# Attention heads on TensorE: mask as contraction rows, output product from high and low halves

## The reference

```python
mask = cid[None, :ke] <= cid[s0:e0, None]           # cid: 0 for meta tokens, then 1 per 64 tokens
sc = jnp.einsum('bqhcd,bkhcd->bhcqk', q[:, s0:e0], k[:, :ke])     # c = 0, 1; d = 64
p = jax.nn.softmax(jnp.where(mask, sc, -jnp.inf), axis=-1)
attn = p[:, :, 0] - lam * p[:, :, 1]
outs.append(jnp.einsum('bhqk,bkhe->bqhe', attn, v[:, :ke]))        # e = 128
```

## Time and profile before

| | us |
|---|---|
| median of 3 runs | 1306.67 (1305.73 to 1308.74) |
| profiled execution, first to last instruction | 1303.2 |
| PE busy | 1278.0 (98%) |
| PE weight loads busy | 1153.7 (89%) |
| DVE busy | 682.4 (52%) |
| ACT busy | 544.9 (42%) |
| POOL busy | 65.8 (5%) |
| attention, from the first scores to the last output product | 674.2 to 900.0 |

### The profile page before, as it was taken

One profiled execution on the slowest core, in us unless ns is written; L12 is line 12 of the kernel. 1 busy time (PEld: TensorE's weight loads), 2 busy tenths in 40 slices (PEclk: granted clock), 3 DMA queues, 4 the chain that ended last, 5 costly groups with the idle time before them and its releaser, 6 DMA issues.

```text
span 1303.2 us, 20870 instructions
## 1 busy us (share of the span) xinstructions
PE 1278.0 (98%) x8381; PEld 1153.7 (89%) x8381; DVE 682.4 (52%) x992; ACT 544.9 (42%) x895; POOL 65.8 (5%) x90
## 2 busy tenths in 40 slices
PE   7999999999999999999999999998999999999997
PEld 6899999999999999999988888876888888888886
DVE  5877777654334334234556677663643343443443
ACT  4656655543214123123445566664532241231332
POOL 3321221000000000000000000000000000000000
PEclk9899999999999999999999999999999999999999
DMA  6352242222232322222321211210332323232311
GB/s 161 84 122 72 65 111 75 71 75 89 96 97 98 98 65 97 97 91 70 97 81 50 65 49 48 64 64 33 97 97 98 97 98 97 97 97 97 97 65 64
DMA packets 141574, 110.28 MB, mean 85 GB/s; under 512 B 22104, under 2 KB 139920, under 8 KB 141520
## 3 DMA queue, kind: packets, MB, share of 16 engines
q1 hardware_dynamic: 140000, 104.93, 26.2%
q0 software_dynamic: 1392, 4.49, 1.5%
q10 hardware_dynamic: 128, 0.09, 0.0%
HBM read 107.38 MB, written 2.13 MB: 84 GB/s over the span
## 4 chain that ended last, share of the span: by engine, by line
issue 53%; PE 42%; DVE 2%; ACT 1%; DMA 0%; POOL 0%; SPq 0%; DVEq 0%; POOLq 0%; ACTq 0%
PE ps L1196 38%; PE ps L1245 2%; PE ps L1262 1%; DMA raw<-in_mlstm_w_in_dram 0%; DVE wl L814 0%; POOL dmat L437 0%; DVE yl L856 0%; PE ps L1315 0%; PE ps L1348 0%; PE ps L1294 0%; ACT wh L461 0%; DVE fin L1178 0%; DVE h L841 0%; PE ps L1212 0%; POOL sql L454 0%
## 5 line engine op out<-in xcount | busy, mean ns | idle before, releaser
L1196 PE MATMUL ps<-yh,wh 128*128 128x264 f32 (+1 forms) x1472 | 368.1, 314 | 0.5 <-DVE wl L814 0.4
L1196 PE MATMUL ps<-yl,wh 128*128 128x264 f32 (+1 forms) x1472 | 361.7, 309 | 0.0
L1196 PE MATMUL ps<-yh,wl 128*128 128x264 f32 (+1 forms) x1472 | 360.8, 309 | 0.0
L461 ACT ACTIVATE wh<-raw 128x1024 fp32r<-128x1024 f32 x192 | 200.1, 1049 | 188.4 <-PE ps L1196 187.9
L814 DVE TENSOR_TENSOR wl<-raw,wh 128x1024 fp32r<-128x1024 f32 x192 | 240.1, 1254 | 55.3 <-ACT wh L461 53.3
L1196 PE MATMUL ps<-ah,wh 128*128 128x264 f32 (+1 forms) x960 | 257.6, 322 | 1.3 <-DVE al L1167 0.8
L1196 PE MATMUL ps<-al,wh 128*128 128x264 f32 (+1 forms) x960 | 257.0, 322 | 0.0
L1196 PE MATMUL ps<-ah,wl 128*128 128x264 f32 (+1 forms) x960 | 256.3, 321 | 0.0
L1196 PEld LDWEIGHTS ps<-yh,wh 128*128 128x128 f32 x1472 | 239.7, 189 | 17.2 <-issue 1.7
L1196 PEld LDWEIGHTS ps<-yh,wl 128*128 128x128 f32 x1472 | 239.2, 189 | 13.7
L1196 PEld LDWEIGHTS ps<-yl,wh 128*128 128x128 f32 x1472 | 239.5, 189 | 13.0 <-issue 0.2
(11 more groups left out here) (196 smaller groups left out, 1072.6 us busy)
## 6 DMA issues: line engine op xcount, KB each, us to landing
raw<-in_mlp_w_up_dram SPq DMA_DIRECT2D x32, 1024.0 KB, 5.2
raw<-in_mlp_w_down_dram SPq DMA_DIRECT2D x32, 1024.0 KB, 4.9
raw<-in_diff_w_in_dram SPq DMA_DIRECT2D x24, 512.0 KB, 3.8
raw<-in_mlstm_w_in_dram SPq DMA_DIRECT2D x16, 512.0 KB, 3.9
raw<-in_mlstm_w_in_dram SPq DMA_DIRECT2D x16, 256.0 KB, 4.1
raw<-in_mlstm_w_out_dram SPq DMA_DIRECT2D x3, 1024.0 KB, 4.9
raw<-in_diff_w_out_dram SPq DMA_DIRECT2D x3, 1024.0 KB, 5.0
mbc<-gate_rows POOLq DMA_DIRECT2D x8, 264.0 KB, 4.5
```

Of the source, the lines that this page charges most:

```text
L461: return nc.scalar.activation(o, i, ACT.Copy, scale=scale)
L1196: last = mm(ps[:, bank + s, 0:w_], w[:, slot, kb, :], m[:, kb, t0:t0 + w_], start=(kb == 0 and n == 0), stop=(kb == CB - 1 and n == 2))
```

## The change

It has two parts, with the buffers and waits that they need.

The scores take two products and no mask row. `qm` holds q's high half on 64 partitions and, on the other 64, rows with -1e30 for the queries of each masked block; `khm` holds the keys' high half and rows with 1 for the keys of that block. `qst` by `klh` (low half and high half of the keys) gives the rest. ACT makes the copy of q once more, for `qm`; DVE's `keys_lo` writes one half in place of two. POOL builds the mask rows once, with two copies on DVE.

The output takes three fp32r products in place of native fp32: `ath`, `atl` for the weights, `vth1`, `vtl1` for the values, and the meta keys in one product of 96 rows that holds all three pairs. DVE makes the low halves from PSUM (`turned_lo`, `values_lo`, `meta_lo`), ACT copies the meta rows twice. Where PE waited for ACT's copy out of PSUM, it now waits for DVE's subtraction behind it (`atl_rd`, `vtl_rd1`, `metal_rd`).

```diff
 # ACT, step1
-                copy(att_meta[:, :], ps[0:NMETA, B_TR1, :]).then_inc(meta_rd, 1)
+                copy(att_meta[0:16, :], ps[0:NMETA, B_TR1, :])
+                copy(att_meta[64:80, :], ps[0:NMETA, B_TR1, :]).then_inc(meta_rd, 1)
...
                         last = copy(qst[1 - par][c][b0:b0 + 64, :], qf1[b0:b0 + 64, NMETA:T], SCORE_SCALE)
                     last.then_inc(qhi_done, 1)
+                    for c in range(2):
+                        b0 = 64 * c
+                        last = copy(qm[1 - par][c][b0:b0 + 64, :], qf1[b0:b0 + 64, NMETA:T], SCORE_SCALE)
+                    last.then_inc(qm_done, 1)
                     split_unit(n1 * 3 + (U_IN1 + 3), 0, 1, n1 + 1)
 # ACT, values
-                    copy(vth1[par][0:16, 4, :], ps[0:16, B_TR1 + 1, 0:P]).then_inc(vt_rd1, 1)
+                    copy(vmeta[par][0:16, :], ps[0:16, B_TR1 + 1, 0:P])
+                    copy(vmeta[par][32:48, :], ps[0:16, B_TR1 + 1, 0:P]).then_inc(vt_rd1, 1)
 # DVE
+            def turned_lo(n, i):
+
+                dve.wait_ge(at_rd, n + 1)
+                V.tensor_tensor(atl[:, 0:i + 1, P * i:P * (i + 1)],
+                                ps[:, B_TR1, 0:P * (i + 1)].rearrange("p (s t) -> p s t", t=P),
+                                ath[:, 0:i + 1, P * i:P * (i + 1)].bitcast(F32), ALU.subtract).then_inc(atl_rd, 1)
+
+            def values_lo(hd, par):
+
+                dve.wait_ge(vt_rd1, hd + 1)
+                V.tensor_tensor(vtl1[par][:, :, :], ps[:, B_TR1, :].rearrange("p (s e) -> p s e", e=P),
+                                vth1[par][:, :, :].bitcast(F32), ALU.subtract)
+                V.tensor_tensor(vmeta[par][64:80, :], ps[0:16, B_TR1 + 1, 0:P],
+                                vmeta[par][0:16, :].bitcast(F32), ALU.subtract).then_inc(vtl_rd1, 1)
+
+            def meta_lo(hd):
+
+                dve.wait_ge(meta_rd, hd + 1)
+                V.tensor_tensor(att_meta[32:48, :], ps[0:NMETA, B_TR1, :],
+                                att_meta[0:16, :].bitcast(F32), ALU.subtract).then_inc(metal_rd, 1)
...
                 if exists(hd):
                     maxima(hd * 4, 0)
+                if exists(hd - 1):
+                    turned_lo(hd * 4 - 1, 3)
+                if exists(hd):
+                    values_lo(hd, par)
                     weights(hd, hd * 4, 0)
                 if exists(n1) and exists(hd):
                     split(n1 * 3 + (U_IN1 + 2), 2)
...
+                if exists(hd - 1):
+                    meta_lo(hd - 1)
                 if exists(hd):
                     maxima(hd * 4 + 1, 1)
                     weights(hd, hd * 4 + 1, 1)
...
+                if exists(hd):
+                    turned_lo(hd * 4, 0)
+                if exists(n1):
                     split(n1 * 3 + (U_IN1 + 3), 0)
...
                     maxima(hd * 4 + 2, 2)
                     weights(hd, hd * 4 + 2, 2)
+                    turned_lo(hd * 4 + 1, 1)
                 if exists(n1):
 
                     scaled(n1 * 3 + (U_IN1 + 1), 0, ALL, kf1[:, :])
...
+                if exists(hd):
+                    turned_lo(hd * 4 + 2, 2)
 # PE
-                        masked = s == len(cuts) - 1
-                        mm(o, q, khs[par][c][:, t0:t0 + w_], start=True, stop=False)
-                        last = mm(o, q, kls[par][c][:, t0:t0 + w_], start=False, stop=not masked)
-                        if masked:
-
-                            last = mm(o[:, w_ - 64:w_], neg_row[:, :], one_row[:, :], start=False, stop=True)
+                        mm(o, qm[par][c][:, tile], khm[par][c][:, t0:t0 + w_], start=True, stop=False)
+                        last = mm(o, qst[par][c][:, tile], klh[par][c][:, t0:t0 + w_], start=False, stop=True)
...
-                wait(pe, at_rd, n)
+                wait(pe, atl_rd, n)
...
-                pe.wait_ge(meta_rd, n + 1)
-                mm(ps[:, B_PV1, :], vth1[par][0:NMETA, 4, :], att_meta[:, :], start=True, stop=False)
+                pe.wait_ge(metal_rd, n + 1)
+                mm(ps[:, B_PV1, :], vmeta[par][:, :], att_meta[:, :], start=True, stop=False)
                 for s in range(4):
-                    last = mm(ps[:, B_PV1, P * s:X], vth1[par][:, s, :], att[:, s, P * s:X], start=False, stop=(s == 3))
+                    for m, (v, w) in enumerate(((vth1, ath), (vth1, atl), (vtl1, ath))):
+                        last = mm(ps[:, B_PV1, P * s:X], v[par][:, s, :], w[:, s, P * s:X], start=False,
+                                  stop=(s == 3 and m == 2))
...
-                pe.wait_ge(vt_rd1, min(n + 2, HEADS) if isinstance(n, int) else n + 2)
-                pe.wait_ge(at_rd, n * 4 + 4)
+                pe.wait_ge(vtl_rd1, min(n + 2, HEADS) if isinstance(n, int) else n + 2)
+                pe.wait_ge(atl_rd, n * 4 + 4)
...
                     pe.wait_ge(qlo_done, n1)
+                    pe.wait_ge(qm_done, n1)
...
-                    wait(pe, at_rd, hd * 4)
+                    wait(pe, atl_rd, hd * 4)
```

More of the change, by code:

```diff
@@ L160, in program @@
         tbuf = new("tbuf", [P, T])
+        abuf_at = cursor[0]
         abuf = new("abuf", [P, T])
@@ L208, in program @@
         w0 = [arena]
-        qf1 = place("qf1", [P, T], F32, w0, limit)
+        vf1 = place("vf1", [P, T], F32, w0, limit)
+        qf1 = vf1
         kf1 = place("kf1", [P, T], F32, w0, limit)
[L211 to L217, removed]
+        s3 = [ring_at + 3 * CB * P * 4], [ring_at + (RING + 3) * CB * P * 4]
+        qm = [[place(f"qm0{c}", [P, X], F32R, s3[0], limit) for c in range(2)],
+              [place(f"qm1{c}", [P, X], F32R, w0, limit) for c in range(2)]]
+        qst = [[place(f"qst0{c}", [P, X], F32R, s3[1], limit) for c in range(2)],
+               [place(f"qst1{c}", [P, X], F32R, w0, limit) for c in range(2)]]
+        z6 = [a_at + 6 * T * 4], [a_at + (CB + 6) * T * 4]
+        khm = [[place(f"khm0{c}", [P, T], F32R, z6[0], a_end) for c in range(2)],
+               [place(f"khm1{c}", [P, T], F32R, w0, limit) for c in range(2)]]
+        klh = [[place(f"klh0{c}", [P, T], F32R, z6[1], a_end) for c in range(2)],
+               [place(f"klh1{c}", [P, T], F32R, w0, limit) for c in range(2)]]
+        vth1 = [place(f"vth1{par}", [P, 4, P], F32R, w0, limit) for par in range(2)]
+        vtl1 = [place(f"vtl1{par}", [P, 4, P], F32R, w0, limit) for par in range(2)]
+        vmeta = [place(f"vmeta{par}", [96, P], F32R, w0, limit) for par in range(2)]
+        att_at = w0[0]
+        ath = place("ath", [P, 4, X], F32R, w0, limit)
+        atl = place("atl", [P, 4, X], F32R, w0, limit)
+        att_meta = place("att_meta", [96, X], F32R, w0, limit)
+        w0_mask = [att_at]
+        qmask = place("qmask", [P, X], F32, w0_mask, limit)
+        kmask = place("kmask", [P, T], F32, w0_mask, limit)
         attn = place("attn", [P, 4, T], F32, w0, limit)
@@ L221, in program @@
         zf = place("zf", [P, X], F32, w0, limit)
-        sqh1, sql1 = (place(n, [P, X], F32R, w0, limit) for n in ("sqh1", "sql1"))
+        sqh1 = place("sqh1", [P, X], F32R, w0, limit)
+        sql1 = place("sql1", [P, X], F32R, [abuf_at + 4 * NMETA], limit)
         hg = place("hg", [P, CB, X], F32, [y_at], y_end)
@@ L1109, in keys_lo @@
                 dve.wait_ge(khi_done, n1 * 2 + (c + 1))
-                for b in (0, 64):
-                    last = V.tensor_tensor(kls[1 - par][c][b:b + 64, :], kf1[64 * c:64 * c + 64, :],
-                                           khs[1 - par][c][0:64, :].bitcast(F32), ALU.subtract)
-                last.then_inc(klo_done, 1)
+                b0 = 64 * c
+                V.tensor_tensor(klh[1 - par][c][b0:b0 + 64, :], kf1[b0:b0 + 64, :],
+                                khm[1 - par][c][b0:b0 + 64, :].bitcast(F32), ALU.subtract).then_inc(klo_done, 1)
+            def turned_lo(n, i):
[13 more added lines that the diff above has]
+                                att_meta[0:16, :].bitcast(F32), ALU.subtract).then_inc(metal_rd, 1)
             def step1(hd, par, pair):
@@ L1509, in step1 @@
                         out_part(1, 0, 1)
-                    wait(pe, meta_rd, hd)
-                    wait(pe, vt_rd1, hd + 1)
+                    wait(pe, metal_rd, hd)
+                    wait(pe, vtl_rd1, hd + 1)
                     turn(hd * 4, 0)
```

54 lines of the change are left out of this document (40 added, 14 removed).

## The result

The change makes the kernel slower: 1331.55 us (median of 4 runs, 1328.93 to 1332.05) against 1306.56 (4 runs), a ratio of 1.0181, 95% interval 1.0164 to 1.0197. The profiled execution went from 1303.2 to 1330.3 us, +27.1, where the sum said +19.5.

What follows compares the result with a forecast made beforehand. The prediction took a ring of waits through PE, DVE and ACT, 31.1 us a head, to replace PE's work as the bound. Its terms sum to +19.5: 1303.2 to 1322.7, plus 3.5 for the median, 1326 us; range 1309 to 1338.

Steps and rivals of the forecast that it cites:

- the ring: Chain of steps through PE, DVE and ACT from one head to the same place in the next: 31.1 us a head.
- The eight links: Steps from DVE's evacuation of q to that of the next head: 9.0, 1.74, 6.79, 2.96, 1.27, 2.67, 2.91, 3.74 us.
- the sixth: From the transposes of the values to `turn_meta`, through ACT's two copies and DVE's `values_lo`: 2.67 us.
- PE's saving: Mask products gone, 2.2 us a head, and a cheaper output product, 1.1: 3.3 us a head, PE's work about 25.0.
- The four waits: PE idle before `scores` 3 (1.5 us), `turn` 2 (1.0), the transposes of the values (2.0) and the output product (1.3).
- From one head to the whole: Heads 2 to 6 +13.8, head 1 +1.5, head 0 +1.5, ahead of it 0.4, last head +2.3: +19.5 us.
- Head 0: First head, with neither `turned_lo` 3 nor an output; only `qm` and `turned_lo` 1 count: +1.5 us.
- the clock falls: Rival: recurring idle gaps in the attention bring PE's clock down, +12 us a head, 1420 us; chance 0.02.
- Ahead of the attention: Before head 0, the second copy of q costs 0.4 us.
- PE as the bound: Rival: PE stays the bound in the attention and the waits fit into slack, -26 us, 1281 us; chance 0.12.
- Links that are covered: Rival: `qm` and `turned_lo` 1 off the ring, perhaps `meta_lo` too: head 29.4 or about 28.1 us, 1305 to 1314; chance 0.11.
- Products of more than one pass: Rival: the output's fp32r products run at the native rate, +5.5 us a head, 1370 us; chance 0.02.

Runs made afterwards that it cites:

- four together: All of the change with `qm` late, meta rows' subtraction earlier, `turned` 1 around block 2's exponentials, `turned_lo` 3 ahead of `maxima` 0: 27.60 us a head, 1299.73 us.
- meta rows early: The changed kernel with `meta_lo` ahead of DVE's split and released by ACT's first meta copy: 30.31 us a head, 1321.67 us.
- the ten products: The changed kernel with ten useless 512-column fp32r products before scores 3 in head 0 only: 1327.34 us, ratio 1.0165 to the kernel before.
- the mask rows alone: The changed kernel with the output back in native fp32, without low halves and their waits: 28.63 us a head, 1308.43 us, ratio 1.0023 to the kernel before.
- the reordered kernel: All of the change with six places reordered, two more in DVE's queue than the kernel with four links shortened: 25.62 us a head, 1286.35 us.
- the mask rows alone and `qm` late: The changed kernel with native fp32 output and ACT's `qm` copies behind its unit of the split: 27.32 us a head, 1297.55 us, ratio 0.9935.

## Why the prediction was right, and where it was off

**The sign, the mechanism and the ring held.** The eight links, forecast and then measured in the rows of head 3 above: from q to the reciprocal 9.0, 8.94; to k 1.74, 1.71; to zf 6.79, 6.64; to `maxima` 0 2.96, 2.96; to the transposes 1.27, 1.22; to `turn_meta` 2.67, 2.94; to the output product 2.91, 2.98; to q 3.74, 3.87. The sums are 31.1 and 31.26. No link is off by more than 0.3; the largest, the sixth, is the values' way through ACT's two small copies and DVE. That the measured links add up to the head is no evidence, they must; what counts is that each came out within 0.3, and that moving single steps then took off 1.34 and 0.96 us, as a ring must. The 3.67 of four together is right in the sum only.

**PE's saving** was right in both parts. The output product measured 2.22 (forecast 2.12) and the masks 2.45 a head (forecast 2.2) once PE was the bound. PE's own work, forecast at 25.0, was 25.62 less the 0.8 of small waits, 24.8.

**The four waits** were forecast at 1.5, 1.0, 2.0 and 1.3 and have brackets of 1.46, 0.77, 1.60 and 1.18. Most of the 0.8 between the sums is a matter of reading: a bracket counts from the modelled end of the product before. Counted from starts the waits are 1.61, 0.93, 1.77 and 1.35, 5.7 us where 5.8 was forecast.

**From one head to the whole** is where the 7.6 us between +19.5 and +27.1 lie:
- Head 0: +4.1 where the sum had +1.5. Its mechanism was among the rivals, as "the clock falls", but taken as all or nothing, at 12 us a head. It came for 7 us and cost 2.3. This is the term that was wrong: the clock must be asked for stretch by stretch.
- Ahead of the attention: +2.9, forecast 0.4. The second copy of q gives the 0.4: PE's wait before its first scores goes from 1.34 to 1.81 us. The other 2.4 arise in code that the change doesn't touch: both profiles have a wait of 1.48 us that ends at 44.2 us, and before the clock fell behind it (from 46 to 52 us), while in the changed kernel it didn't, but fell behind a wait of 2.41 us at 56.1 and stayed at 0.50 from 58 to 64 us, where PE had no gap. Two kernels with the same work up to there, meta rows early and the ten products, start their scores at 674.20 and 673.85, where the changed kernel has 677.10 and the kernel before 674.22, so it is the execution and not the change. How often the late fall comes isn't known: the changed kernel's other executions lasted 1327.3 to 1330.4 us.
- Heads 2 to 6: +14.8, forecast 13.8. Head 1: +2.15, forecast 1.5. The last head: +3.1, forecast 2.3, and from 904 to 908 us its clock is at 0.57, behind a wait of 1.90 us.

**Around the span** the sum took the 3.5 us by which the median of before lay above the profiled span. That was too much: in the changed kernel an execution takes 1.6 us more than its span, and the rest of the 3.5 was that the profiled execution of before was a short one (1303.2 + 1.6 is 1304.8, below the shortest of the four runs, 1305.73). By medians the change costs 25.0 us, the sum said 19.5, and this step gave 2 us back.

**The rivals.** PE as the bound: the most contended engine, which the Trainium skill ("Perfetto Trace Analysis", "Identifying the Most-Contended Engine") has one relieve first, was indeed PE here; the run with the mask rows alone took over 2 us a head of work off it and got slower. The trace disagrees with the rule as a forecast of the gain, and agrees with it once the order is changed: then the same relief is worth 2.45 us a head. Links that are covered: none was. Products of more than one pass: 0.23 us for 512 columns (778.35 to 778.58 in PE's timeline). The oscillation that the Trainium skill ("TensorE: Matmul & The Clock Gate", "HAM oscillation") warns of doesn't appear in heads 2 to 6: with 5 us of waits in every head the windows stay at 1.00. The falls in head 0 and in the last head stand behind the two longest waits that the changed kernel has in the attention, 2.54 and 1.90 us.

What stays open: what brings the clock down behind one wait and not behind another of the same length. Nor was it tried what the reordered kernel gives with its last 0.8 us of waits gone.

## What to carry to other kernels

When an engine is busy without a gap, its neighbours' idle time isn't slack until the ring through all of them has been added up: here one copy of 1.3 us was enough to make the ring the bound, and nearly every step that the change put on it came back as wait. Work given to an idle engine has to be placed by who waits behind it in that engine's queue: the same `qm` copy cost 1.3 us a head ahead of the weights' rounding and nothing behind it (with the mask rows alone and `qm` late, q to the reciprocal is 7.65 us; it was 7.64 in the kernel before), and six such moves turned +1.8% into -1.5% with no instruction less. Before judging a change made of two parts, run each alone in the best order: the mask part carried all but 0.25 us a head of the gain.

## What the runs showed of the hardware

- The granted clock falls behind single waits, and not always. In head 0 six of the thirteen profiles have it at 1.2 GHz, for 3 to 7 us. Behind a wait of 2.5 us it fell in three of three kernels, behind 1.8 us in two of four, behind waits of 1.2 to 1.4 us before scores 0 or scores 3 in two of six, and once behind 1.1 us. In the last head it fell in all four kernels with a wait of 1.9 us before the output product (in one of them shortly before that wait ended), in one of three with 0.9 us, and not with 1.5 us. What settles it was not found. In heads 2 to 6 of the changed kernel waits of up to 1.6 us, 5 us in 31, left it at 1.00. While it was low, a pair of 264-column products took 0.44 us instead of 0.24.
- DVE's instructions ran 10 to 40% longer beside GpSimd's copies: 0.70 to 0.85, 0.77 to 1.09 and 1.23 to 1.36 us. By GpSimd's rows (767.15 to 768.43, 775.70 to 776.32, 777.81 to 778.44) each got longer by about half of the time that it shared with the copy, which is an estimate, since GpSimd's spans are rough.
- A bracket of 0.23 us or none at all stood where PE lost 0.2 to 0.3 us between two starts. For waits below half a microsecond, compare the distances of starts between two kernels.
